# High parts of the weights one eviction earlier, low parts behind the eviction, a gate's norm factor at its eviction, and four transposes before the state-space loop

## The reference, cut to what matters

```
def mlp(h, g, w_up, w_down):                 # every layer
    n = rmsnorm(h, g)
    return h + (relu(n @ w_up) ** 2) @ w_down
def ple(h, p, g, w_proj, w_gate):            # every layer, "per-layer embedding"
    return h + (p @ w_proj) * sigmoid(rmsnorm(h, g) @ w_gate)
layer 0: h = h + attention_and_gla(rmsnorm(h)); h = mlp(h); h = ple(h, p[0])
layer 1: h = h + glu(gelu(state_space(rmsnorm(h)))); h = mlp(h); h = ple(h, p[1])
```

## Time and profile before

| | |
|---|---|
| time, median of three runs | 1163.2 us (1162.53 to 1164.2) |
| the profiled execution's own time | 1163.06 us |
| its span between first and last instruction | 1161.4 us |
| PE busy in the span | 1078.4 us, 93% |
| DVE, ACT, POOL busy | 545.8, 414.8, 138.8 us |

### The profile page before, as it was taken

One profiled execution on the slowest core, in us unless ns is written; L12 is line 12 of the kernel. 1 busy time (PEld: TensorE's weight loads), 2 busy tenths in 40 slices (PEclk: granted clock), 3 DMA queues, 4 the chain that ended last, 5 costly groups with the idle time before them and its releaser, 6 DMA issues.

```text
span 1161.4 us, 16430 instructions
## 1 busy us (share of the span) xinstructions
PE 1078.4 (93%) x6346; PEld 899.5 (77%) x6346; DVE 545.8 (47%) x954; ACT 414.8 (36%) x711; POOL 138.8 (12%) x236
## 2 busy tenths in 40 slices
PE   6998979999999789788999998989999899999988
PEld 5996446567655458788977776769999899999987
DVE  5433665464453423865430004255666355564443
ACT  5422444431122223455240004322465355453343
POOL 3440000000133230000210007700000000000000
PEclk9997979897799989999999999965599899999999
DMA  7456001110335423434432331040034244333330
GB/s 304 161 170 256 1 1 46 64 46 19 106 123 153 146 82 109 159 131 145 146 131 109 122 145 73 1 190 1 1 134 177 109 156 171 146 143 148 146 155 31
DMA packets 33758, 135.26 MB, mean 116 GB/s; under 512 B 5257, under 2 KB 16777, under 8 KB 21010
## 3 DMA queue, kind: packets, MB, share of 16 engines
q1 hardware_dynamic: 26786, 116.71, 27.7%
q0 software_dynamic: 6896, 17.51, 4.5%
HBM read 130.04 MB, written 4.17 MB: 116 GB/s over the span
## 4 chain that ended last, share of the span: by engine, by line
PE 68%; DVE 15%; ACT 10%; issue 5%; POOLq 1%; DMA 1%; POOL 1%; DVEq 0%; ACTq 0%
PE ps L807 17%; PE ps L776 8%; PE ps L967 7%; PE ps L778 7%; PE ps L777 7%; DVE ring_split L1702 5%; ACT hi_split L1347 3%; PE ps L1237 2%; PE ps L1245 1%; PE ps L1252 1%; PE ps L1251 1%; ACT up_hi_split L1347 1%; ACT a2hi_split L1654 1%; PE ps L970 1%; DVE arena L2018 1%
## 5 line engine op out<-in xcount | busy, mean ns | idle before, releaser
L967 PE MATMUL ps<-arena 128*128 128x512 f32 x256 | 150.7, 680 | 0.0
L807 PE MATMUL ps<-arena,ring 128*128 128x288 f32 x512 | 125.1, 406 | 0.0
L807 PEld LDWEIGHTS ps<-arena,ring 128*128 128x128 f32 x512 | 97.2, 190 | 26.8
L1702 DVE TENSOR_TENSOR ring_split<-ring,hi_split 128x2048 fp32r<-128x2048 f32 x36 | 82.3, 2292 | 56.6 <-ACT hi_split L1347 56.6
L776 PE MATMUL ps<-nhi_split,hi_split 128*128 128x288 f32 x320 | 98.0, 306 | 10.1 <-DVE arena L2018 6.5
L970 PEld LDWEIGHTS ps<-arena 128*128 128x128 f32 x256 | 51.9, 203 | 68.1 <-issue 68.1
L778 PE MATMUL ps<-nhi_split,ring_split 128*128 128x288 f32 x320 | 96.2, 301 | 0.0
L776 PE MATMUL ps<-up_nhi_split,up_hi_split 128*128 128x288 f32 x256 | 77.5, 303 | 14.1 <-DVE arena L2011 14.1
L1835 DVE TENSOR_REDUCE arena<-arena 128x8 f32<-128x512 f32 x64 | 43.5, 684 | 82.5 <-ACT arena L1422 82.5
L776 PE MATMUL ps<-a2hi_split,hi_split 128*128 128x288 f32 x256 | 76.0, 297 | 1.5 <-DVE ring_split L1702 1.2
L777 PE MATMUL ps<-up_lo_split,hi_split 128*128 128x288 f32 x256 | 76.6, 299 | 0.0
(11 more groups left out here) (375 smaller groups left out, 2390.2 us busy)
## 6 DMA issues: line engine op xcount, KB each, us to landing
ring<-in_stream SPq DMA_DIRECT2D x97, 1024.0 KB, 4.9
arena<-in_ckvT SPq DMA_DIRECT2D x64, 128.0 KB, 2.0
arena<-in_ckv POOLq DMA_DIRECT2D x49, 128.0 KB, 2.6
arena<-in_wu POOLq DMA_DIRECT2D x1, 2176.0 KB, 10.0
arena<-in_s POOLq DMA_DIRECT2D x4, 512.0 KB, 4.0
out_gla_s<-arena POOLq DMA_DIRECT2D x4, 512.0 KB, 2.9
arena<-in_ckv SPq DMA_DIRECT2D x15, 128.0 KB, 2.5
hT<-in_x SPq DMA_DIRECT2D x2, 576.0 KB, 4.2
```

Of the source, the lines that this page charges most:

```text
L807: mm = pe.matmul(ps[base:base + m, 0:T], wv[:, k, col:col + m], rhs(k), start=first and k == 0, stop=last and k == blocks - 1)
L967: mm = pe.matmul(ps[:, :], pages[:, p % 4, j, k], wuk[:, k], start=k == 0, stop=k == KB - 1)
L1702: V.tensor_tensor(lo_parts[slot][:, :], ring[slot][:, :], as_whole(hi_part(v)[:, :]), ALU.subtract).then_inc(unit_split, 1)
```

## The change

Eight edits, all to the order in which work is done or to where a factor is applied; the result is the same function.

1. Layer 0 up: the high part of a unit is asked for one group earlier on ACT, and on DVE the low part stands behind the eviction of its group in place of ahead of it.
2. Layer 1 up: the same, and on top of it one more high part and one more low part stand before the norm's factor rs.
3. The norm of layer 0's embedding sums its squares in pairs on DVE, so that PE does two matmuls (`sumsq_of_two(2)`) in place of eight.
4. The norm's factor rs is no longer multiplied into n (eight DVE instructions behind rs): DVE forms n = h * g inside the down projection, and multiplies each gate by rs at its eviction, as layer 1 does already. ACT's sigmoid then works from SBUF.
5. The first four lag products come directly behind the down projection, the other four behind the first gate.
6. The transposes 0 to 11 come three behind each of the gates 1 to 4, and 12 to 15 between the last gate and the state-space loop.
7. The first products of layer 1's embedding are in plain order: gate 0 is completed ahead of proj 1 and gate 1.
8. Its third high part comes right behind rs, its fourth behind the second gate's sigmoid; the low parts behind gates 0 and 2.

```diff
-LATE = (1, 4, 5)
+LATE = (1, 2, 4, 5)
...
 def turns(i):
-    return range(3 * i + 1 if i else 0, min(3 * i + 4, 16))
+    return range(3 * i - 3, 3 * i) if 1 <= i <= 4 else range(0)
...
-                    if i >= 2:
-                        sumsq_part(2, i - 2)
                 lag_products(0)
-                sumsq_part(2, 6)
-                sumsq_part(2, 7)
-                lag_products(4)
...
                     project(("proj", L, i), wp, P * i, P, D, lambda k: p3[:, k], blocks=2)
+                    if i == 0:
+                        sumsq_of_two(2)
...
                     project(("gate", L, i), w, P * (i % 2), P, 256, nk, norm_wait(2 + 3 * L) if i == 0 else None)
+                    if i == 0:
+                        lag_products(4)
...
+            b_turned(12)
+            b_turned(13)
             sumsq_part(3, 7)
+            b_turned(14)
+            b_turned(15)
...
             def squared_up(L, i):
                 if L == 0:
-                    hi_unit(min(U["up0_0"] + i // 2 + 2, U["up0_15"]))
+                    hi_unit(min(U["up0_0"] + (i + 1) // 2 + 2, U["up0_15"]))
                 copied(act, ("up", L, i))
...
-            gates(0, [("gate", 0, i) for i in range(8)], before=turned_b_and_square)
+            normed_gates(0, [("gate", 0, i) for i in range(8)], before=turned_b_and_square)
             turned_b_and_square(8)
+            turned_re(12)
             rsqrt(rsi, ("ss", 3), width=J)
+            turned_re(14)
...
+            hi_unit(U["up1_0"] + 3)
             rsqrt(rs[:, :], ("ss", 4))
...
             for i in range(FB):
-                hi_unit(U["up1_0"] + i // 2 + 2)
+                hi_unit(U["up1_0"] + (i + 1) // 2 + 3)
                 squared_up(1, i)
...
                 for i in which:
-                    lo_unit(min(U["up0_0"] + i // 2 + 2, U["up0_15"]))
                     ps = result(dve, ("up", L, i))
                     V.scalar_tensor_tensor(a2[:, i], ps[:, 0:T], 0.0, rs[:, :], ALU.max, ALU.mult).then_inc(bank_of(("up", L, i)), 1)
+                    lo_unit(min(U["up0_0"] + i // 2 + 2, U["up0_15"]))
...
-                    lo_unit(U["up1_0"] + i // 2 + 2)
                     ps = result(dve, ("up", 1, i))
                     V.scalar_tensor_tensor(a2[:, i], ps[:, 0:T], 0.0, rs[:, :], ALU.max, ALU.mult).then_inc(bank_of(("up", 1, i)), 1)
+                    lo_unit(U["up1_0"] + i // 2 + 3)
...
-            add_to_h([("down", 0, i) for i in range(8)])
+            for i in range(8):
+                add_to_h([("down", 0, i)], i)
+                copied(dve, ("down", 0, i))
+                V.tensor_scalar(n3[:, i], h3[:, i], prm("g_ple0")[:, i:i + 1], None, ALU.mult).then_inc(n_ready, 1)
+                if i in (4, 6):
+                    add_squares(2, i // 2 - 2)
...
-                if i == 3:
-                    norm(2, prm("g_ple0"))
...
             add_squares(4, 2)
+            lo_unit(U["up1_0"] + 2)
             copied(dve, ("ss", 4))
```

More of the change, by code:

```diff
@@ L225, in plan @@
         if L == 0:
[L226 to L238, removed]
+            for i in range(3):
+                g.add(("G", i), "side", 4, 4 + i)
+            main(("G", 3), 4)
+        g.add(("ss", 2 + 3 * L), "side", 1, 7)
+        for i in range(8):
             main(("proj", L, i))
@@ L241, in plan @@
             if L == 0:
+                if i == 0:
+                    for k in range(4, 8):
+                        g.add(("G", k), "side", 4, k)
                 for n in turns(i):
-                    g.add(("BT", n), "side", 1, 4 + (n + 2) % 3 if n else 7)
+                    g.add(("BT", n), "side", 1, 4 + n % 3)
                 if 5 <= i:
                     g.add(("u", i - 5), "side", 1, i - 1)
+        if L == 0:
+            for n in range(12, 16):
+                main(("BT", n))
     return g
@@ L1192, in ple @@
                     w = split_unit(f"gate{L}_0")
-                    for i in range(2):
-                        project_split(("proj", L, i), wp, P * i, D, lambda k: (phi[:, k], plo[:, k]), blocks=2)
[L1195 to L1202, removed]
+                    project_split(("proj", L, 0), wp, 0, D, lambda k: (phi[:, k], plo[:, k]), blocks=2)
+                    project_split(("gate", L, 0), w, 0, 256, nsplit, split_wait(4), blocks=range(7), last=False)
+                    sumsq_of_two(5)
+                    project_split(("gate", L, 0), w, 0, 256, nsplit, split_wait(4), blocks=range(7, 8), first=False)
+                    for i in range(1, 8):
+                        project_split(("proj", L, i), wp, P * i, D, lambda k: (phi[:, k], plo[:, k]), blocks=2)
+                        if i and i % 2 == 0:
                             w = split_unit(f"gate{L}_{i // 2}")
@@ L1255, in _ @@
             for i in range(-3, 8):
+                if i + 3 == 4:
+                    for n in range(12, 16):
+                        copied(pe, ("BT", n))
                 if i + 3 < 8:
@@ L1571, in _, with lag_matrices @@
             act.wait_ge(toep_zero, 1)
-            for i in range(8):
+            def lag_matrices(i):
                 ps = result(act, ("G", i))
@@ L1578, in _ @@
                                    ACT.Copy).then_inc(bank_of(("G", i)), 1)
+            for i in range(4):
+                lag_matrices(i)
                 if i == 1:
@@ L1669, in _ @@
             rsqrt(rs[:, :], ("ss", 5))
-            normed_gates(16, [("gate", 1, i) for i in range(8)], lambda i: hi_unit(U[f"gate1_{min(i // 2 + 2, 3)}"]) if i % 2 else None)
+            hi_unit(U["gate1_2"])
+            normed_gates(16, [("gate", 1, i) for i in range(8)], after=lambda i: hi_unit(U["gate1_3"]) if i == 1 else None)
         @block.vector
@@ L2145, in _, with lag_diagonals @@
                             ALU.mult).then_inc(d_ready, 1)
+            add_squares(2, 2)
             dve.wait_ge(toep_zero, 1)
-            for i in range(8):
+            def lag_diagonals(i):
                 ps = result(dve, ("G", i))
@@ L2214, in _ @@
                 normed_inputs(i)
+            turned_im(15)
             for i in range(9):
@@ L2295, in _ @@
             copied(dve, ("ss", 5))
-            gated(16, [("proj", 1, i) for i in range(8)], [("gate", 1, i) for i in range(8)], after=lambda i: lo_unit(U[f"gate1_{min(i // 2 + 2, 3)}"]) if i % 2 else None,
+            gated(16, [("proj", 1, i) for i in range(8)], [("gate", 1, i) for i in range(8)], after=lambda i: lo_unit(U[f"gate1_{i // 2 + 2}"]) if i in (0, 2) else None,
                   normed=True)
```

37 lines of the change are left out of this document (28 added, 9 removed).

## The result

The changed kernel takes 1099.69 us (median of four runs, 1098.73 to 1106.48); the kernel before took 1162.87 beside it (four runs). The ratio is 0.9472, 95% interval 0.943 to 0.9513: 63 us less, where 39.7 had been forecast and 1110 us was the lower end of the range. The profiled execution took 1098.73 us with a span of 1097.1.

The account below looks back on a forecast made before the run. PE, busy for 93% of the span, was taken as the bound. Gains of 12.3 + 11.3 - 0.65 + 11.6 + 5.1 = 39.65 us from 1163.06 gave 1123.4 us, range 1110 to 1140.

Parts of the forecast that it names:

- I take the loop itself as unchanged: State-space loop: PE's 74.90 us of work at clock 0.50 was expected to stay, with no gain counted.
- second rival: State-space loop: transposes fill part of the gap ahead, so the clock stays up; 20 us more, 1103 us, chance 0.06.
- Waits of the same kind stay: Argument against the raised clock: ahead of the loop, waits of about 1.9 and 0.8 us remain after the transposes.
- Through 75 us of small matmuls the clock never rose: Argument against the raised clock: the loop ran its whole length at clock 0.50 in the profile before.
- a term of 1.75 us: Layer 0's embedding start: four transposes leave PE's path for waits before the loop, gaining 1.75 us at full clock.
- Layer 0 up: Layer 0's up projection: opening the ring of high part, low part, eviction and square gains 12.3 us, leaving 3.8 of waits.
- the first rival: Up projections: high parts asked for earlier find their slot or load no sooner; 1143.3 us, chance 0.13.
- a sign of being wrong: Failure sign: PE waits for DVE's low parts, which now stand behind evictions; no size given.
- Start of the embedding and of the loop: Layer 0's embedding start gains 11.3 us, from waits, matmuls, transposes and clock; the start of the state-space loop loses 0.65.
- Layer 1's up and down: Layer 1's projections: 3.95 us of the first wait, 6.4 in the up stage and 1.24 at the down go; sum 11.6.
- The tail: Kernel's end: gate 0's sigmoid begins about 1.6 us sooner, waits and half clock shrink, 2.0 us of waits stay; gain 5.1.
- POOL's rotation factors: Slower rival: the 49.40 us chain, with 7.6 us to spare before the loop, comes too late; chance 0.02.

Follow-up runs that it names:

- the kernel without fill: Changed kernel with transposes 12 to 15 moved behind gates 5 and 6, nothing new between last gate and state-space loop: 1122.78 us, ratio 0.9672.
- the two kernels before with fill: Kernel before, gap ahead of the loop given transposes 12 to 15 (1143.54 us) or four groups of identity transposes nobody reads (1146.11 us).
- the three kernels with fill in them: Changed kernel plus unread matmuls ahead of loop waits: 12, 22, 12 in steps 5 to 7 (1101.27 us); 7, 13, 2 (ratio 0.9483); five steps (1097.97 us).
- fill at all five of the long waits: Changed kernel plus 4, 6, 7, 13 and 2 unread matmuls in loop steps 0, 1, 5, 6 and 7: 1097.97 us, ratio 0.9449.
- fill at the loop's end alone: Changed kernel plus 7, 13 and 2 unread matmuls in loop steps 5, 6 and 7: 1097.64, 1108.79, 1114.47 and 1097.7 us, ratio 0.9483.

## Why the prediction was wrong

**The step that failed** is "I take the loop itself as unchanged". The loop lost 23.0 us, because it began at the upper clock. The forecast had that case as its second rival, priced it at 20 us and 1103, and gave it 0.06. Two arguments stood against it, and both were misread. "Waits of the same kind stay": they did, 1.73 and 0.46 where 1.9 and 0.8 had been worked out, but the trace of before showed only that 3.7 us of idle time in this gap let the clock fall; it said nothing on 2.2. "Through 75 us of small matmuls the clock never rose": true, and the kernel without fill shows it again (74.89 us at 0.50). But whether a stretch of work lifts the clock and whether it holds one that is up are two questions; the same loop at the upper level held it for 39 us in the changed kernel and for all 50 with fill.

The small chance came also from counting the moved transposes as a term of 1.75 us that the waits "cover". Work that is moved into a gap is free on the path; what it does to the engine's clock behind the gap was the larger effect by far, and the row with 74.90 us at 0.50 had shown how much was at stake.

Transposes were enough to hold the clock here: both kernels in which nothing but float32 transposes was added to the gap of the kernel before entered the loop at 1.00 (24.68 and 22.90 us of it), where that kernel ran it at 0.50. The Trainium skill (TensorE: Matmul & The Clock Gate, section Part 4: PE-mode transpose) says that transposes do not count as activity for the clock as matmuls do. In so far as that would leave them without effect, these runs differ from it and the measurement decides; that they count for as much as matmuls, or would raise a clock that is down, no run here shows.

**The terms that held.** Layer 0 up: stage of 93.68 us for 93.8. Groups of the changed kernel from 466.3 to 560.2, which answer to the earlier trace rows:

```profile
L774 PE MATMUL ps<-up_nhi_split,up_hi_split 128*128 128x288 f32 x224 | 66.8, 298 | 4.4 <-DVE ring_split L1722 2.4 <-DVE arena L2030 2.0
L1722 DVE TENSOR_TENSOR ring_split<-ring,up_hi_split 128x2048 fp32r<-128x2048 f32 x13 | 29.7, 2281 | 0.4 <-ACT up_hi_split L1348 0.4
L1348 ACT ACTIVATE up_hi_split<-ring 128x2048 fp32r<-128x2048 f32 x13 | 24.8, 1911 | 8.8 <-PE ps L776 8.7
```

PE's idle time fell from 14.1 to 4.4 us, and the low parts' wait for high parts from 27.9 to 0.4. The high parts now wait 8.7 us for PE to free their slots, as the first rival said; but they are so far ahead that low parts wait only those 0.4 us for them. Of PE's 4.4 us, 2.4 are waits for low parts, which the forecast had named as a sign of being wrong. They are 0.24, 1.67 and 0.50 us long, and answer to the 0.5, 1.9 and 0.8 that it had worked out for three units, so they are part of the sum and no failure of it.

Start of the embedding and of the loop: 10.3 for 10.65. The one new wait, for the diagonal, is 0.41 us for 0.3; the gap from the last gate to the loop is 5.40 us for 4.85, a loss of 0.55 for 0.65. One part of that 0.65 was misread: ACT's copy of a transpose has 512 columns and takes 0.58 us, not 0.2 from 128 columns. It costs next to nothing, because it lies beside the last sum of squares (PE, to 742.6), which rs has to wait for anyway. ACT in the changed kernel:

```profile
742.14 0.58 ACT L1605 ACTIVATE arena<-ps 128x512 f32<-128x512 f32 x1
742.68 0.32 ACT L1329 ACTIVATE rs<-ps,eps 128x72 f32<-128x72 f32 x1
```

Layer 1's up and down: 12.5 for 11.6. The 4.16 us wait is gone altogether, and PE is busy for 101.27 of 101.35 us. The tail: 6.1 for 5.1; waits of 0.32 and 0.80 us stay where 2.0 had been left, and the clock is 1.00 throughout. In both stages the forecast kept waits back that did not come. These parts give the same alone (18.9 for the layer-1 edits), so they did not live on the raised clock.

POOL's rotation factors did not come late: they were done at 733.4, 10.7 us ahead of the loop's start. Their chain took 48.9 us for 49.4 before, so the shortening by up to 3.6 us that the forecast considered was 0.5.

Two sums beside the forecast's own are off, and neither touches it: the upper bounds add up to 46.6 us and 1116.5, not 48 and 1115, and POOL's chain would have to reach 99.0 us in all (49.4 + 7.6 + 42), not 91.6.

**What stays open.** Where inside the loop the clock falls. It fell 25 and 23 us behind the loop's start in the two kernels before with fill, and 39 us in both profiled executions of the changed kernel, with like waits up to there; and runs of one kernel differ (1098.7 at a mean clock of 0.953, 1106.5 at 0.940). That the loop's waits for DVE take part is likely: the three kernels with fill in them kept 1.00 to the loop's end in the profiled execution, and with fill at all five of the long waits no run had a mean clock below 0.954. But fill at the loop's end alone left two runs of four at 0.944 and 0.939. Where the clock fell in those, and what decides between executions, was not tried.

## What to carry to other kernels

Where a stage shows 100% busy at clock 0.50, look at the idle time just ahead of it before anything in it: here two waits of 3.7 us in all cost 23 us behind them, and four groups of transposes in them, useful or not, brought all or part of it back. That the clock never rose in the loop was no evidence that it would fall there: a trace at one level of the clock does not say what the same work would do at the other, and a rival worth 20 us deserves a closer look than a chance of 0.06. And orders in which an eviction waits behind preparation for later work can be costed step by step: three such terms came out within 1 us.

## What was not expected of the hardware

- The step is sharp: with 3.2 us of idle time in the gap the loop took 74.5 to 74.6 us, with 2.2 us 51.87. Nothing between the two was tried.
- Useless work pays: the kernel before took 0.9875 of its time with transposes added that nobody reads.
- Fill inside the loop lifted the stage to clock 1.00 throughout (50.04 us) and changed the whole by nothing that can be told from the runs: of the 1.8 us the GLU took 1.0 back, with a fall of the clock of its own.
